# Skewed units, three job banks, x loaded already transposed, and one hand-set order of calls for all units behind the first

## What is computed

```python
h = rms_norm(x, norm_gain)
proj = jnp.einsum('bsd,de->bse', h, w_in)              # 1024 -> 5632 columns
aq, ak, av, ag, rq, rk, rv, rg = jnp.split(proj, SPLIT_POINTS, axis=-1)
attn = window_attention(aq, ak, av, q_norm_gain, k_norm_gain, sink_logits)
#   16 heads of 64 on 4 k/v heads, QK-norm, ALiBi bias, a sink per head,
#   each 64-chunk sees itself and the chunk before it
ret = retention(rq, rk, rv, ret_norm_gain)
#   8 heads, qk 64, v 128: decayed q k^T inside, a running state across, GroupNorm
mixed = jnp.concatenate([attn * jax.nn.silu(ag), ret * jax.nn.silu(rg)], axis=-1)
x = x + jnp.einsum('bse,ed->bsd', mixed, w_out)
```

## Time and profile before

| | |
|---|---|
| median of 3 runs | 1658.88 us (1658.84 to 1659.61) |
| the profiled execution, its own time | 1657.89 us |
| its span, first to last instruction | 1656.1 us |
| PE busy in it | 1598.1 us (96%) |
| VectorE, ScalarE, GpSimd busy | 1166.8, 673.7, 450.8 us |
| units 0 to 3: from one unit's first Q job to the next one's | 108.6, 107.5, 107.5, 111.1 us |
| units 4 to 14, those without and with the next block's x | 98.6 and 103.1 us |

### The profile page before, as it was taken

One profiled execution on the slowest core, in us unless ns is written; L12 is line 12 of the kernel. 1 busy time (PEld: TensorE's weight loads), 2 busy tenths in 40 slices (PEclk: granted clock), 3 DMA queues, 4 the chain that ended last, 5 costly groups with the idle time before them and its releaser, 6 DMA issues.

```text
span 1656.1 us, 24605 instructions
## 1 busy us (share of the span) xinstructions
PE 1598.1 (96%) x8320; PEld 1380.1 (83%) x8320; DVE 1166.8 (70%) x3045; ACT 673.7 (41%) x1985; POOL 450.8 (27%) x453
## 2 busy tenths in 40 slices
PE   5999999999999999999999999999999999999999
PEld 5778788787798888888888898888888888888887
DVE  6887768867868576684776757576686766757576
ACT  6543635535444242432444334241444414334241
POOL 5546446454412111121211212121121111212111
PEclk9999999999999999999999999999999999999999
DMA  9748567575774443546357353443547445353451
GB/s 309 280 147 309 200 215 267 185 249 206 245 293 145 176 180 125 200 156 216 125 196 286 135 203 139 170 191 118 213 171 267 181 173 189 129 203 133 171 197 51
DMA packets 151453, 320.49 MB, mean 194 GB/s; under 512 B 26272, under 2 KB 89888, under 8 KB 151328
## 3 DMA queue, kind: packets, MB, share of 16 engines
q1 hardware_dynamic: 151328, 318.91, 53.9%
HBM read 247.56 MB, written 71.30 MB: 193 GB/s over the span
## 4 chain that ended last, share of the span: by engine, by line
PE 51%; DVE 29%; ACT 13%; issue 5%; POOL 1%; DMA 0%; SPq 0%; DVEq 0%; ACTq 0%
PE jb L902 15%; PE jb L904 15%; PE jb L903 14%; ACT sx L417 6%; DVE sx L632 3%; DVE m L635 3%; DVE sx L630 2%; DVE qS L610 2%; DVE d L640 2%; DVE pTL L560 1%; DVE rawqn L603 1%; DVE rawqn L600 1%; ACT qS L400 1%; POOL rstd L303 1%; PE s L975 1%
## 5 line engine op out<-in xcount | busy, mean ns | idle before, releaser
L902 PE MATMUL jb<-wH,hTH 128*128 128x512 f32 (+1 forms) x1024 | 373.8, 365 | 0.0
L903 PE MATMUL jb<-wL,hTH 128*128 128x512 f32 (+1 forms) x1024 | 372.0, 363 | 0.0
L904 PE MATMUL jb<-wH,hTL 128*128 128x512 f32 (+1 forms) x1024 | 371.9, 363 | 0.0
L902 PE MATMUL jb<-wH,mxH 128*128 128x512 f32 x512 | 206.7, 404 | 10.8 <-DVE mxL L560 10.7
L904 PEld LDWEIGHTS jb<-wH,hTL 128*128 128x128 f32 x1024 | 192.8, 188 | 20.5
L902 PEld LDWEIGHTS jb<-wH,hTH 128*128 128x128 f32 x1024 | 193.4, 189 | 18.6
L903 PEld LDWEIGHTS jb<-wL,hTH 128*128 128x128 f32 x1024 | 193.0, 188 | 18.2
L902 PE MATMUL jb<-hTH,wH 128*128 128x512 f32 x512 | 203.4, 397 | 4.0 <-DVE gate L653 4.0
L903 PE MATMUL jb<-hTL,wH 128*128 128x512 f32 x512 | 201.2, 393 | 0.0
L904 PE MATMUL jb<-hTH,wL 128*128 128x512 f32 x512 | 201.1, 393 | 0.0
L904 PE MATMUL jb<-wH,mxL 128*128 128x512 f32 x512 | 200.6, 392 | 0.0
(11 more groups left out here) (148 smaller groups left out, 2973.6 us busy)
## 6 DMA issues: line engine op xcount, KB each, us to landing
wH<-scrH SPq DMA_DIRECT2D x144, 512.0 KB, 7.4
wL<-scrL SPq DMA_DIRECT2D x144, 512.0 KB, 8.1
scrH<-wH SPq DMA_DIRECT2D x48, 512.0 KB, 5.3
scrL<-wL SPq DMA_DIRECT2D x48, 512.0 KB, 6.0
wH<-scrH SPq DMA_DIRECT2D x48, 384.0 KB, 5.8
wL<-scrL SPq DMA_DIRECT2D x48, 384.0 KB, 6.5
stage<-w_in_dram SPq DMA_DIRECT2D x64, 256.0 KB, 4.5
acc<-x_dram SPq DMA_DIRECT2D x4, 2048.0 KB, 15.2
```

What stands on the lines that cost most here:

```text
L902: pe.matmul(o, lh, rh_, start=i == 0, stop=False)
L903: pe.matmul(o, lh, rl_, start=False, stop=False)
L904: m = pe.matmul(o, ll, rh_, start=False, stop=i == last)
```

## The change

The diff is a rewrite of all five engine programs. What it does:

- **Skew.** The O phase of unit n-1 stands between Q and G of unit n. `phases(n)` gives Q, G, V for unit 0; Q(n), O(n-1), G(n), V(n) for units 1 to 14; Q, G, V, O(14), O(15) for the last. The steps A(3), I(2), I(3) and MT of unit n-1 move into the Q phase of unit n and the O phase behind it; TQ, S, PT(0) of unit n stand in the O phase.
- **Three job banks.** `bank_of` uses three in turn, and a job waits for the job three before it. For that TQ writes bank `ob` (shared with PV) and MT writes `ab` (shared with A), each with new waits.
- **Tables of steps.** `STEPS_FIRST` for unit 0, `STEPS_MID` for units 1 to 14, `STEPS_LAST`; on the other engines the calls are written out in `qkv_phase` and `late_phases`, the same for units 1 to 14.
- **x.** The host hands over x also transposed (`xT`). The tiles are loaded that way into `xt`, and `h` on VectorE multiplies each with the gain and with the row factor, which TensorE spreads (`XB`, one transpose a tile instead of eight). `xh` is two ScalarE instructions a tile instead of eight; `xl` moves from VectorE to GpSimd for blocks 1 to 3. The squares come from a second load of x in rows (`x_rows`, `xsq`), two tiles in the O phase of the block's unit 1 and two in that of its unit 2.
- **Weights.** The host packs each panel, so a chunk is one DMA instead of up to three. `stage` has three chunks instead of four. The save of a chunk is issued with the load of the chunk three behind it.
- In units 1 to 3 (and for O of unit 3 in unit 4) the splitting stands at other places: O's panel in the Q phase, G's panel in the O phase behind each `exps`.
- Small: `qS` has 2 slots instead of 4; `ms`, `rstd`, `m4`, `den` and others have 2 slots instead of 1; `oraw` has 2 slots and takes over `mr`; the first block's mask is a memset; the squares of block 0 are as before.

```diff
-STAGES = 4
+STAGES = 3
...
+def phases(n):
+
+    if n == 0:
+        return [("Q", 0), ("G", 0), ("V", 0)]
+    if n < LAST:
+        return [("Q", n), ("O", n - 1), ("G", n), ("V", n)]
+    return [("Q", n), ("G", n), ("V", n), ("O", n - 1), ("O", n)]
...
+STEPS_MID = {("Q", 0): [("A", -1, 3)], ("Q", 1): [("I", -1, 2), ("MT", -1, 0)], ("Q", 2): [("I", -1, 3)],
+             ("Q", 3): [("TQ", 0, 0), ("MT", -1, 1)],
+             ("O", 1): [("TQ", 0, 1)], ("O", 2): [("S", 0, 0), ("MT", -1, 2)], ("O", 3): [("TQ", 0, 2)],
+             ("O", 4): [("S", 0, 1), ("MT", -1, 3)], ("O", 5): [("TQ", 0, 3)], ("O", 6): [("PT", 0, 0)],
+             ("O", 7): [("S", 0, 2)], ("G", 0): [("PV", 0, 0)], ("G", 1): [("PT", 0, 1), ("S", 0, 3)],
...
-        jb = [pb("jb0"), pb("jb1")]
-        tr, ptb, ob, ab = pb("tr"), pb("ptb"), pb("ob"), pb("ab")
+        jb = [pb("jb0"), pb("jb1"), pb("jb2")]
+        ptb, ob, ab = pb("ptb"), pb("ob"), pb("ab")
+        tr = ob
...
+            def qkv_phase(n):
+
+                m = n - 1
+                rvg(m, 3); kw_am(m, 3); rl(m, 2); gnv(m, 1)
+                if n % NU == 0:
+                    h(n // NU, 3)
+                gnb(m, 1)
+                qkv(n, 0); rupd(m, 2); rl(m, 3); gna(m, 2); kwl_al(m, 3); gnv(m, 2); mtl(m, 0)
+                qkv(n, 1); gnb(m, 2); rupd(m, 3); gna(m, 3); carry_in(n); gnv(m, 3)
+                qkv(n, 2); tql(n, 0); mtl(m, 1); gnb(m, 3)
...
+                qkv(n, 3); tql(n, 1); add(m, 0); mtl(m, 2); part1(n, 0); add(m, 1)
+                tql(n, 2); add(m, 2); part1(n, 1); add(m, 3); mtl(m, 3); part2(n, 0)
+                tql(n, 3); add(m, 4); ptl(n, 0); part2(n, 1); add(m, 5)
...
+                exps(n, 0); wh(n, 1, (0, 1))
+                tqh(n, 2); mth(n - 1, 3); exps(n, 1); wh(n, 1, (2, 3))
+                if b < NB - 1 and u in (1, 2):
+                    xsq(b + 1, 2 * (u - 1))
+                    xsq(b + 1, 2 * (u - 1) + 1)
+                tqh(n, 3); pth(n, 0); exps(n, 2); wh(n, 1, (4, 5))
+                if b < NB - 1 and u == 3:
+                    xrb_copy(b + 1)
+                wh(n, 1, (6, 7))
...
-            def XT(b, t):
+            def XB(b, t):
+
+                pe.wait_ge(S["s_xr"], nth(b, 4, t))
+                if b and t == 0:
+                    ab_free()
+                bank = ab[:, t * P:(t + 1) * P] if b else xbanks[t][:, 0:P]
+                pe.transpose(bank, xr[:, t:t + 1].broadcast_to([P, P]), ident[:, :]).then_inc(S["s_xb"], 1)
```

1005 lines of the change are left out of this document (600 added, 405 removed), and 15 rows, old and new, of tables (STEPS_FIRST, STEPS_LAST, STEPS_MID).

## The result

| | before | after |
|---|---|---|
| median | 1659.16 us (1658.84 to 1659.61, 4 runs) | 1783.68 us (1779.82 to 1786.45, 4 runs) |
| profiled execution: own time, span | 1657.89, 1656.1 us | 1782.84, 1781.0 us |
| mean granted clock | 0.996 | 0.969 |

The ratio is 1.0749 (95% interval 1.0728 to 1.077). The prediction said 1676, range 1625 to 1702: the sign is right, the size is 7 times too small (17 us against 124.5).

A forecast was written before the change was run, and what follows sets the result against it. TensorE, busy 96% of the span, was taken as the bound. Start and units 0 to 3 came to 433.3 us, units 4 to 15 to 1238.2, the end to 3.7: span 1675.2, median 1676, range 1625 to 1702.

The forecast's parts named there:

- The plain unit: Units without extra work: 97.5 us of TensorE work plus waits of 1.1 (I(3)) and 0.65 (PT(0)), 99.3 instead of 98.6.
- The squares: Units 1, 2, 5, 6, 9, 10: two squares ahead of tqh(3) delay O job 7, 1.5 us more.
- The turn: Units 4, 8, 12: h(3) adds eight rows in the Q phase, gpow(1) stands behind two xl pieces; 2.7 us taken.
- The G panel's order: Units 1 to 3: the last four wh stand behind exps(2), delaying the first G job; 4.5 us each.
- VectorE held in block 0: Q and O phases: GpSimd's splitting holds one or two rows per QK-norm; waits 7.3 us a unit instead of 1.8.
- TQ(1) 2.6: Block 0's units: TQ(1) comes 2.6 us late because GpSimd holds VectorE rows.
- The start: Unit 0: third tile of xT lands at 23 to 25 us, Q phase ends at 37.8 instead of 43.3.
- The last unit: Unit 15 with both O phases: 97.5 + 25.3 + 3 for waits, 125.8 us; the end behind the last matmul 3.7.
- The clock: Part of a slower rival: block 0's mean clock 0.97 to 0.98, half speed after TensorE waited about 1.9 us in short sequence.
- VectorE falls behind for good: Slower rival: rpow and ggm hold VectorE in all 15 units' Q phases, held h adds 5 us a turn; 1705, chance 0.14.
- The slack wins: Faster rival: VectorE runs ahead by some 2.5 us, TQ(1), TQ(3), PT(0) no longer wait; 1627 us, chance 0.28.

The follow-up runs named there:

- the three moves: Changed kernel with VectorE's group for I(3) ahead of qkv(n,0), ScalarE's kwh_ah(3) ahead of ocopy(2) and rh(3), PT(0) at O job 7: 1750.0 us.
- mended order: Changed kernel with I(3) and PT(0) moves, late squares and xpow, early G pieces, rpow(2) and gpow(0) moved: 1719.1 us; without splitting 1663.9 us.
- the pauses: Changed kernel with TensorE made to wait on GpSimd's clears of a small tile in G phases of units 5 to 14: 1801.2 us.
- all 14 variants: The follow-up kernels made from the changed kernel by altering orders, loads, splitting or pauses; spans from 1662 to 1798 us.

## Why the prediction was wrong, step by step

The span was forecast at 1675.2 us and came to 1781.0. By the terms of the sum:

| stretch | forecast, us | measured, us | more |
|---|---|---|---|
| up to unit 1 | 98.8 | 120.2 | 21.4 |
| units 1 to 3 | 334.5 | 373.9 | 39.4 |
| unit 4 | 108 | 116.8 | 8.8 |
| units 5, 6, 9, 10 | 403.2 | 407.5 | 4.3 |
| units 7, 11, 13, 14 | 397.2 | 405.2 | 8.0 |
| units 8, 12 | 204 | 214.2 | 10.2 |
| unit 15 and the end | 129.5 | 143.2 | 13.7 |

The direction was right, and most of the places where TensorE would newly wait were named. Two steps failed. The first is the price of a wait: the sum took each at its own length and the lower clock at nothing, and by the balance the clock is 48 of the 125 us. The second is the list of waits in block 0, at the turns, at the start and in the last unit. It made VectorE late only by single held rows, and TensorE's waits went from 36.4 to 138.7 us. The steps one by one:

- **The plain unit, 99.3.** It took 100.4. Both named waits are there, and nothing else: I(3) 1.16 us (predicted 1.1, though the walk's own terms give 0.9), PT(0) 1.33 to 1.38 (predicted 0.65), and with the three moves both went. Own work is 98.0 (the 98.4 with the moves, less its 0.4 of wait), not 97.5, so each unit was 0.5 us too short in the sum, 8 us in all.
- **The squares, 1.5.** Measured 1.5. Right in place and size.
- **The turn, 2.7.** Units 8 and 12 took 107.1, 6.7 over a plain unit. "The turn to the next block" priced `h(3)` as eight unheld rows and left its follow-up out: held by `xl` they took 3.3 us, the `aL` behind them 1.49 instead of 0.42, I(3) then waited 5.4, and 6.8 us at the lower clock stand there. The rule that the prediction weighed (the Trainium skill, SBUF — State Buffer, section Who interferes with whom) holds for this pair: eight rows with the factor in SBUF took 3.30 us beside `xl`, with the factor in PSUM 2.15 even beside a `wL` piece. The hold was put aside as a risk of the V phase. There it was larger (`h(2)` took 4.75 us) and the V phases of units 7 and 11, 27.2 us as in a plain unit, hid it; it struck in the Q phase.
- **The G panel's order, 4.5 a unit.** The order of `wh` is worth some 3 to 4 us, in two units. The walk's own times gave 3.2 (56.5 for 53.3) and 3.9 (63.0 for 59.1); the 4.5 taken from them was too much. What held unit 2 was another line of the same kind that I did not see: four `xpow` ahead of the panel's `wl` on GpSimd. With it and the squares out of the way that unit became 11.8 us shorter.
- **VectorE held in block 0, 7.3 a unit.** In units 1 to 3 "TQ(1) 2.6" was 3.5 us each time, I(3) 1.35, 3.67 and 3.68 instead of 1.2, PT(0) 1.8, 1.4 and 1.35 instead of 2.1; in unit 4 I(3) waited 8.4. The places are right, and these three sum to 6.6, 8.6 and 8.5 us, near the 7.3. Waits of other steps are missing: PV's in these units (10 us in all), and I(2)'s of 4.9 us in unit 1 and 2.4 in unit 4. But the step assumed that the splitting costs what it did before. It costs 56 us instead of 30 (with and without, in both kernels), and in mended order still 55. That it now stands in the phases where VectorE has the least slack is my reading; the runs show the price and not the reason.
- **The start, 37.8.** The Q phase ended at 50.2, and G and V took 70.0 instead of 61. The walk counted only when x lands, and had that nearly right: the third Q job started at 26.2 us, 1.8 ahead of the 28. It left out that `carry_in` waits 3.5 us for the sinks ahead of `h(3)`, and that TQ(0), the fourth job and TQ(1) wait for VectorE, 2.8, 2.2 and 7.6 us. Together that is 12.6, and the Q phase ended 12.4 later than forecast. Mending that moved the wait into G. With it went the saving of 12 us from the earlier first job.
- **The last unit, 125.8 + 3.7.** It took 143.2. No step was walked there. 10.2 us at the lower clock lie in it ahead of the last matmul, and the waits ahead of A (3.5 us) and PV (3.2 us) alone are more than the 3 us that the sum allowed.
- **The clock.** The prediction had it in a rival only, at 0.97 to 0.98 as read in the old block 0. It fell to 0.90 in unit 0 and to 0.92 to 0.94 in units 1 to 4. By the balance it is 48 of the 125 us; it is the largest term that the sum did not have. A list of waits that are each priced at themselves is too low once some are long: the pauses show it for 3.84 us against 1.26. That waits close together do the same was not tried by itself.
- **The rivals.** "VectorE falls behind for good" named three mechanisms that are in the traces: held rows, `h` beside `xl`, the clock. It had 0.14 and 1705; it priced each by itself. "The slack wins" had 0.28: with five orders mended the plain unit came out at 98.3, as that rival says, and block 0 did not.

What stays open: why unit 0 takes 104.6 to 108.0 us from its first Q job to unit 1's in all 14 variants. Its V phase takes 41.4 us (38.1 to 41.4 in the variants) where a plain one takes 27.2; three waits sum to 6.8, the granted clock of 0.87 from 80 to 120 us stands for about 5 more, and 2 are left. Open too is what the skew is worth by itself: of the change's parts only the transposed x ran alone. The third bank, the three stages and the packed loads were never taken apart from the skew.

## What to carry to other kernels

When work moves to another place in an order, price two things before the sum: what the helpers on other engines (splitting, powers) hold up while they run there, and what the clock does behind the sum of the waits. A call that waits for a late producer (here xpow, exps, h) delays all that stands behind it on its engine, so look at what each such call has behind it. And try the parts of a large change one by one: here one part in the old order gained 7 us, and all of them together cost 125.

## What I had not expected of the hardware

- A pause of 3.84 us in otherwise full TensorE work made one G phase 6.7 us longer and the next unit's 5.7, with 6.8 and 3.4 us at the lower clock; one of 1.26 us cost 1.5 and no clock.
- The price of lateness is stable: span less waits less half of the time at the lower clock came to 1581 to 1593 us in the changed kernel and all its 14 variants.
- A VectorE row of 128 partitions and two SBUF inputs was held beside a GpSimd row for up to about 1.1 us (`aL` 1.49 for 0.42), and a group of eight such rows several times over: `h` of a tile took 2.18 to 5.37 us. With one input in PSUM it was not held at all (eight rows of `h`, 2.15 us, in unit 0 beside `wL`, as without it).
